# Eight modulation slots as raw matmul products between the mixing output and the feed-forward

## The reference, cut to what matters

```
mod = (silu(c) @ w_mod + b_mod)          # w_mod: 2048 x 12288
sh1, sc1, gt1, sh2, sc2, gt2 = split(mod, 6)
h  = rmsnorm(x) * (1 + sc1) + sh1        # ... mixing: recurrences, gates
x  = x + gt1 * (y @ w_out)               # "mixing output"
h2 = rmsnorm(x, g_norm2) * (1 + sc2) + sh2
u_gate, u_val = split(h2 @ w_up, 2)      # "up", 2 x 5504 columns
x  = x + gt2 * ((silu(conv3x3(u_gate) + conv_b) * u_val) @ w_down)   # "down"
```

## Time and profile before

| | |
|---|---|
| median of 3 runs | 2628.92 us (2626.74, 2628.92, 2629.05) |
| the profiled execution's own time | 2626.53 us |
| its span, first to last instruction | 2624.7 us |
| mean granted clock of TensorE | 0.993 |
| mixing output (16 slots) | 594.6 to 686.0 us of the span |
| `up` (86 slots) | 694.1 to 1175.9 us |
| `down` (44 slots) | from 1175.9 us |

### The profile page before, as it was taken

One profiled execution on the slowest core, in us unless ns is written; L12 is line 12 of the kernel. 1 busy time (PEld: TensorE's weight loads), 2 busy tenths in 40 slices (PEclk: granted clock), 3 DMA queues, 4 the chain that ended last, 5 costly groups with the idle time before them and its releaser, 6 DMA issues.

```text
span 2624.7 us, 41249 instructions
## 1 busy us (share of the span) xinstructions
PE 2567.7 (98%) x15774; PEld 2229.0 (85%) x15774; DVE 1987.9 (76%) x3108; ACT 1322.2 (50%) x1973; POOL 0.2 (0%) x4
## 2 busy tenths in 40 slices
PE   5999999999899999999999999999999999999999
PEld 2687778888788888888888888888888998988888
DVE  4587888978988888888556777777654889567577
ACT  3334434455555555553444544445444655676564
POOL 0000000000000000000000000000000000000000
PEclk8999999999999999999999999999999999999999
DMA  9876675426555555558555555555555444543543
GB/s 399 357 311 259 242 290 206 147 73 243 189 192 184 185 190 192 187 184 314 190 189 185 194 192 187 184 189 193 195 185 187 171 171 178 195 142 117 194 170 134
DMA packets 114256, 530.36 MB, mean 202 GB/s; under 512 B 8224, under 2 KB 8768, under 8 KB 65232
## 3 DMA queue, kind: packets, MB, share of 16 engines
q1 hardware_dynamic: 110448, 507.54, 53.2%
q10 hardware_dynamic: 3680, 21.05, 2.2%
HBM read 526.46 MB, written 2.10 MB: 201 GB/s over the span
## 4 chain that ended last, share of the span: by engine, by line
PE 71%; DVE 8%; ACT 3%; issue 1%; ACTq 0%; DVEq 0%
PE ps L2299 43%; PE ps L2300 22%; DVE lo L1307 3%; ACT hi L622 1%; PE ps L2292 1%; PE ps L2291 1%; PE ps L2290 1%; PE ps L2736 1%; PE ps L2562 0%; ACT p L1263 0%; DVE R L2020 0%; DVE O L2018 0%; PE ps L2596 0%; PE ps L2599 0%; DVE R L2059 0%
## 5 line engine op out<-in xcount | busy, mean ns | idle before, releaser
L1307 DVE TENSOR_TENSOR lo<-raw,hi 128x1024 fp32r<-128x1024 f32 x700 | 827.8, 1221 | 387.9 <-ACT hi L622 387.6
L622 ACT ACTIVATE hi<-raw 128x1024 fp32r<-128x1024 f32 x700 | 709.2, 1055 | 637.0 <-PE ps L2300 605.2
L2299 PE MATMUL ps<-x,hi 128*128 128x512 f32 x1376 | 330.6, 392 | 4.7 <-DVE x L1813 4.7
L2299 PEld LDWEIGHTS ps<-x,hi 128*128 128x128 f32 x1376 | 253.6, 189 | 54.4 <-issue 4.9
L2299 PE MATMUL ps<-y,hi 128*128 128x512 f32 x1024 | 250.6, 392 | 0.7 <-DVE y L1727 0.6
L2299 PE MATMUL ps<-xp,hi 128*128 128x512 f32 x1024 | 244.7, 391 | 0.1
L646 ACT ACTIVATE hi<-raw 128x1024 fp32r<-128x1024 f32 x98 | 103.0, 1058 | 231.8 <-DMA raw<-in_weights 94.2
L2299 PEld LDWEIGHTS ps<-xp,hi 128*128 128x128 f32 x1024 | 188.2, 188 | 36.7 <-ACT hi L622 0.3
L2299 PEld LDWEIGHTS ps<-y,hi 128*128 128x128 f32 x1024 | 186.1, 189 | 35.6 <-issue 1.0
L2300 PEld LDWEIGHTS ps<-x,lo 128*128 128x128 f32 x1376 | 177.1, 192 | 7.0
L2300 PE MATMUL ps<-x,lo 128*128 128x256 f32 x1376 | 179.1, 283 | 0.0
(11 more groups left out here) (396 smaller groups left out, 4197.2 us busy)
## 6 DMA issues: line engine op xcount, KB each, us to landing
raw<-in_weights SPq DMA_DIRECT2D x453, 1024.0 KB, 4.8
wlast<-in_weights ACTq DMA_DIRECT2D x16, 1024.0 KB, 6.0
spare<-in_weights SPq DMA_DIRECT2D x13, 1024.0 KB, 22.2
over_squares<-in_weights SPq DMA_DIRECT2D x9, 1024.0 KB, 16.8
xf<-in_xt SPq DMA_DIRECT2D x4, 1024.0 KB, 9.4
raw<-in_weights SPq DMA_DIRECT2D x4, 768.0 KB, 4.3
R<-in_xt ACTq DMA_DIRECT2D x1, 2048.0 KB, 7.3
out<-R SPq DMA_DIRECT2D x1, 1024.0 KB, 8.6
```

The source lines that it names most:

```text
L622: act.activation(HI[p % PAIR][:, c], RAW[p % RING][:, c], ACT.Copy).then_inc(hi_ready, 1)
L1307: dve.tensor_tensor(LO[p % PAIR][:, c], RAW[p % RING][:, c], HI[p % PAIR][:, c].bitcast(F32), ALU.subtract).then_inc(lo_ready, 1)
L2299: return pe.matmul(o, h, pair[:, :, k, :], start=start, stop=False, **kw)
```

## The change

Groups 12 and 13 (eight slots of gt2) are no longer summed by VectorE. The eight slots go into eight buffers of their own (`wdirect`), each loaded by ScalarE's queue in a turn of its own of the mixing output (`DIRECT_TURNS`). TensorE multiplies them raw, as in `mod_slot`, with a second copy of the window tile (`cwin_again`, made by VectorE in turn 0), into bank 7: two slots ahead of `sum_squares`, six behind it, ahead of `up`. ScalarE copies the bank to `mrows_again` once the operands of `up` are made; `turn_rows(4, mrows_again)` stands ahead of the third slot of `up` and writes to bank 6. VectorE adds the bias at the head of its part of `down`, behind `gp`, and TensorE waits for this at the head of the first slot of `down`, since that slot writes bank 6. `column_sums(12)`, `column_sums(13)` and the two `later_modulation` calls behind the operands go away. The other eight slots are done in `down` as before, numbered anew.

```diff
+DIRECT, LAST = FINAL[:8], FINAL[8:]
+DIRECT_TURNS = (1, 2, 4, 5, 7, 8, 10, 11)
...
+            def load_direct(i):
+                act.dma_start(wdirect[i][:, :], A["weights"][MOD_AT + DIRECT[i]]).then_inc(sem(f"last_loaded{i // 4}"), 16)
...
-            load_final(0)
-            load_final(1)
             split("mix_out", 0, 0)
             for u in range(16):
                 if u:
                     split("mix_out", u // RING, u % RING, 2, range(1 if u == 15 else 2))
-                if u - 1 in FINAL_TURNS[:6]:
-                    load_final(FINAL_TURNS.index(u - 1) + 2)
+                if u in DIRECT_TURNS:
+                    load_direct(DIRECT_TURNS.index(u))
...
+            act.wait_ge(sem("whole_used"), len(WHOLE) + 8)
+            act.activation(mrows_again[:, :], PS[7][:, :], ACT.Copy).then_inc(sem("mod_rows"), 1)
             def ff_silu(j, b):
...
                 if u:
                     n2_sum(u - 1)
-                if u in FINAL_TURNS:
-                    i = FINAL_TURNS.index(u)
-                    final_sum(i)
+                if u == 0:
+                    window(cwin_again)
...
-            later_modulation(12)
-            later_modulation(13)
             own.done(dve.memset(pad[0][:, :], 0.0))
...
+            dve.wait_ge(sem("mod_turned"), 5)
+            for g in range(2):
+                j = 80 + 4 * g
+                dve.tensor_tensor(mview[:, j:j + 4, 0], PS[6][:, 0:32].rearrange("p (q w) -> p q w", w=8)[:, :, 2 * g], v("b_mod", j, 4),
+                                  ALU.add).then_inc(sem("mods_ready"), 1)
             for s in range(4 * DOWN_SLOTS):
...
-            sum_squares("n2", "steps")
-            column_sums(12)
-            column_sums(13)
+            def direct(i):
+                pe.wait_ge(sem(f"last_loaded{i // 4}"), 64)
+                for m in range(4):
+                    lo = (4 * (i % 4) + m) * MW + 2 * (3 - i // 4)
+                    ins = pe.matmul(PS[7][32 * m:32 * m + 32, :], cwin_again[:, lo:lo + 32], wdirect[i][:, 512 * m:512 * m + 512],
+                                    start=i == 0, stop=i == 7, skip_group_check=True)
+                ins.then_inc(sem("whole_used"), 1)
+
+            pe.wait_ge(sem("fold_ready"), 4)
+            pe.wait_ge(sem("mods_ready"), 4 + len(GROUP_ENDS))
+            for i in range(8):
+                if i == 2:
+                    sum_squares("n2", "steps")
+                direct(i)
             for i, r in turns(pe, 2 * KF, lead=1):
...
+                if isinstance(i, int) and i == 0 and r == 2:
+                    turn_rows(4, mrows_again)
...
             for s in range(4 * DOWN_SLOTS):
                 q, j = s // DOWN_SLOTS, 4 * (s % DOWN_SLOTS)
                 units = min(4, KF - j)
+                if s == 0:
+                    pe.wait_ge(sem("mods_ready"), 4 + 14)
```

More of the change, by code:

```diff
@@ L54 @@
 FINAL = [u for u in MODS[7] if u not in SUMMED]
-FINAL_TURNS = (2, 4, 5, 7, 8, 10, 11, 13)
+DIRECT, LAST = FINAL[:8], FINAL[8:]
+DIRECT_TURNS = (1, 2, 4, 5, 7, 8, 10, 11)
 MW = 38
@@ L354, in build @@
                 wk("wsum4", 512, 56), wk("wsum5", 512, 58), wk("wsum6", 512, 112), wk("wsum7", 512, 114)]
-        wlast = [wk("wlast0", SLOT, 0), wk("wlast1", SLOT, 8), wk("wlast2", SLOT, 96), wk("wlast3", SLOT, 104)]
+        wdirect = [wk(f"wdirect{i}", SLOT, (102, 110)[i] if i < 2 else 8 * (i - 2)) for i in range(8)]
+        cwin_again = wk("cwin_again", KD * MW, 48)
+        mrows_again = wk("mrows_again", 512, 51)
+        wlast = [wk("wlast0", SLOT, 96), wk("wlast1", SLOT, 104)]
         tmpx2 = wk("tmpx2", T, 101)
@@ L897, in load_final @@
                     act.wait_ge(sem("mod_summed"), 4 * (NSUM + i) - 4)
-                act.dma_start(wlast[i % 2 + (2 if i >= 8 else 0)][:, :], A["weights"][MOD_AT + FINAL[i]]).then_inc(sem(f"last_loaded{i % 2}"), 16)
+                act.dma_start(wlast[i % 2][:, :], A["weights"][MOD_AT + LAST[i]]).then_inc(sem(f"last_loaded{i % 2}"), 16)
+            def load_direct(i):
+                act.dma_start(wdirect[i][:, :], A["weights"][MOD_AT + DIRECT[i]]).then_inc(sem(f"last_loaded{i // 4}"), 16)
             act.wait_ge(sem("operand_rest"), reached("x", "y", 4))
-            load_final(0)
-            load_final(1)
             split("mix_out", 0, 0)
@@ L973, in _ @@
             act.wait_ge(halves_used, 2 * BASE["down"])
-            load_final(8)
-            load_final(9)
+            load_final(0)
+            load_final(1)
             act.wait_ge(sem("gp_ready"), 1)
@@ L979, in _ @@
                 if 1 <= s < 7:
-                    load_final(s + 9)
+                    load_final(s + 1)
                 q, k = s // DOWN_SLOTS, s % DOWN_SLOTS
@@ L1389, in later_modulation @@
             def later_modulation(g):
-                dve.wait_ge(sem("sums_taken"), g // 2 * 2 + 2 if g >= len(GROUP_ENDS) else g + 1)
+                dve.wait_ge(sem("sums_taken"), len(GROUP_ENDS) + 2 if g >= len(GROUP_ENDS) else g + 1)
                 j = 32 + 4 * g
@@ L1395, in multiplied_sum @@
             def multiplied_sum(i, k, w, pieces):
-                total = sums_of(i // 4)
+                total = sums_of(i // 4 + (len(DIRECT) // 4 if i >= NSUM else 0))
                 for m in pieces:
@@ L1517, in _, with window @@
             dve.memset(ones[:, :], 1.0).then_inc(sem("ones_ready"), 1)
-            own.done(dve.memset(cwin[:, :], 0.0))
-            own.wait()
+            def window(t):
+                own.done(dve.memset(t[:, :], 0.0))
+                own.wait()
+                dve.tensor_copy(t[:, :].rearrange("p (k w) -> p k w", w=MW)[:, :, 6:8],
+                                csil[:, :].rearrange("p (k s) -> p k s", s=2)).then_inc(sem("fold_ready"), 1)
             dve.wait_ge(sem("c_act"), 1)
-            dve.tensor_copy(cwin[:, :].rearrange("p (k w) -> p k w", w=MW)[:, :, 6:8],
-                            csil[:, :].rearrange("p (k s) -> p k s", s=2)).then_inc(sem("fold_ready"), 1)
+            window(cwin)
             dve.wait_ge(sem("eye_loaded"), 16)
@@ L1773, in final_sum @@
             def final_sum(i):
-                dve.wait_ge(sem(f"last_loaded{i % 2}"), 16 * (i // 2 + 1))
-                multiplied_sum(NSUM + i, FINAL[i], wlast[i % 2 + (2 if i >= 8 else 0)], range(4))
+                dve.wait_ge(sem(f"last_loaded{i % 2}"), 64 + 16 * (i // 2 + 1))
+                multiplied_sum(NSUM + i, LAST[i], wlast[i % 2], range(4))
             def n2_sum(u):
@@ L1905, in _ @@
                 if s < 8:
-                    final_sum(s + 8)
+                    final_sum(s)
                 q, k = s // DOWN_SLOTS, s % DOWN_SLOTS
@@ L2457, in mod_slot, with turn_rows @@
                 ins.then_inc(sem("whole_used"), 1)
-            def turn_rows(r):
+            def turn_rows(r, rows=mrows):
                 pe.wait_ge(sem("mod_rows"), r + 1)
@@ L2463, in turn_rows @@
                     for m in range(4):
-                        ins = pe.matmul(PS[6 + r % 2][32 * m:32 * m + 32, 8 * q:8 * q + 8], mrows[:, q * P + 32 * m:q * P + 32 * m + 32],
+                        ins = pe.matmul(PS[6 + r % 2][32 * m:32 * m + 32, 8 * q:8 * q + 8], rows[:, q * P + 32 * m:q * P + 32 * m + 32],
                                         fold[:, :], start=True, stop=True, skip_group_check=True)
@@ L2470, in column_sums @@
                 pe.wait_ge(sem("mods_ready"), 4 + (g // 2 * 2 if g >= len(GROUP_ENDS) else g))
-                pe.wait_ge(sem("mod_summed"), 16 * g + 16)
+                pe.wait_ge(sem("mod_summed"), 16 * (g - (len(DIRECT) // 4 if g >= 14 else 0)) + 16)
                 for q in range(4):
```

## The result

The changed kernel takes 2639.65 us (median of 6 runs, 2638.09 to 2641.59), the kernel before 2628.80 (6 runs): ratio 1.0044, 95% interval 1.0034 to 1.0054, 10.9 us slower. A few single executions of one or the other kernel in the runs of this study took 3.6 to 8.7 ms; they are left out everywhere, the profile of one of them too (the first of the sums put back, which records a granted clock of 1.00 and not the low one that the expectation for its repeat names).

The account below looks back on a forecast made before the run. The prediction took TensorE, at work for 98% of the span, as the bound. Its terms, -0.4 + 0.5 + 9.0 + 2.1 = +11.2 us on the median 2628.9, gave 2640 us, range 2635 to 2644.

Parts of the forecast that it names:

- The sum: Whole kernel: -0.4 + 0.5 + 9.0 + 2.1 = +11.2 us, giving 2640.
- The wait at the head of `down`: First slot of `down`: TensorE stalls for VectorE's bias add, 9.0 us, bounds 8.8 to 9.6.
- The clock behind it: First products of `down` after the stall: low granted clock costs 2.1 us, bounds nothing to 4.2.
- The turn: Third slot of `up`: 16 small products outside any hole cost 0.5 us.
- The earlier operands: Gap ahead of `up`: sum of squares at full clock brings the operands 0.4 us earlier, a gain of 0.4.
- The relief of VectorE: Mixing output: taking 24 us of sums off VectorE gains 0, since TensorE never waits for `LO` there.
- VectorE's chain as the gate: First slot of `up`: VectorE's unbroken work sets when blocks 4 to 7 are ready, so TensorE stands still 2.1 us.
- The rival that I priced too low: First slot of `up`: clock falls in the new 2.1 us hole, adding 2.1 us, 2642.2; chance 0.08.
- The two cited rules: Start of `up`: clock rule alone would give back 2.1 us; third slot: without the drain rule, 0.2 us lower.
- the regained clock: Start of `up`: full clock behind the filled gap gains nothing at the end, as TensorE then waits for VectorE.

Follow-up runs that it names:

- the sums put back: The changed kernel with the bias add moved to the fourth slot of `up` and 32 useless VectorE sums in the old eight mixing output turns; ratio 1.0004.
- the add moved: The changed kernel with VectorE's bias add in the fourth slot of `up`, not at the head of `down`; 2628.74 us, ratio 1.0005.
- the wait alone: The kernel before with one line added: TensorE waits for VectorE's `gp` at the head of the first slot of `down`; 2638.59 us, ratio 1.0041.
- the add first: The changed kernel with VectorE's bias add directly behind the last rest of `up`, ahead of the memsets, `eps2` and `gp`; 2639.94 us, ratio 1.0045.
- the `LO` half moved: The changed kernel with the bias add in `up`'s fourth slot, `turn_rows` ahead of block 4, and VectorE's `LO` half two parts later; 2626.63 us, ratio 0.9994.
- `LO` later on before: The kernel before with only VectorE's 1.2 us `LO` half moved two parts later among the operands of `up`; ratio 0.9999.

## Why the prediction was right, and where it was not

*The sum.* Forecast +11.2 us and 2640; measured +10.9 and 2639.65, and 11.6 between the two profiles. The interval of the ratio reaches from 8.9 to 14.2 us, so that the two numbers lie 0.3 apart is luck; what the profiles bear out is the large terms.

*The wait at the head of `down`*: forecast 9.0, measured 8.98, and shown to be the cause from both sides (the add moved: 1.0005; the wait alone: 1.0041). What it rests on was read rightly: VectorE's order behind the last channel block, at the very times of the earlier trace rows plus 0.2. One bound was off: with adds that cost nothing the stall is 1184.55 - 1175.88 = 8.7 us, not 8.8, and the wait alone measured 8.70.

*The clock behind it*: forecast 2.1, measured 2.38 in the changed kernel, 2.2 in the wait alone, 1.9 in the add first, and gone from the profile once TensorE is kept at work.

*The turn*: forecast 0.5, measured 0.46 (from the last narrow group to the wide products of the third slot it is 708.37 - 706.96 = 1.41 us, where the kernel before has 0.95). In the hole it is free.

*The earlier operands*: forecast -0.4, and the profile has -0.37. As a term it was too generous: it counts only for executions of the kernel before in which the clock had fallen ahead of the sum of squares, and two of the three profiles that have nothing filled into that hole show it full there.

*The relief of VectorE* at 0 is borne out by the sums put back. *VectorE's chain as the gate* is borne out by the `LO` half moved: 1.1 us.

*The rival that I priced too low* is the clock falling behind the new 1.8 us hole. Five profiles have this hole unchanged; four of them show the fall, at 1.6 us each, and the one of the changed kernel, which was the fastest of its six runs, does not. The price (2.1 forecast) and the hole's length (2.1 forecast, 1.8 measured) were near enough, the chance of 0.08 was not. The case that the prediction priced it by, the fall at 688 behind a hole of 2.0 us, is itself one of three: in the wait alone and in `LO` later on before, with the same hole, the clock held until 690, by when TensorE stood in the next one. How often it happens over many runs stays open, and so does how the median can be only 10.9 us up if it is frequent: the scatter from stages that the change doesn't touch is as large.

*The two cited rules.* That activity keeps the clock up (the Trainium skill, TensorE: Matmul & The Clock Gate, Part 1) agrees with the traces: 1.00 from 694 to 698, where before had 0.50. The four falls behind a hole of 1.8 us, which is not a long one, it does not lead one to expect; there the measurement decides. What the prediction held against it stands too: the regained clock ran into the wait for VectorE, 1.81 us, instead of shortening anything. The drain between tiling modes (the Trainium skill, TensorEngine Tiling (Array Packing), Key Properties) can only lie within the 0.46 us of the turn; no run here shows it apart.

## What to carry to other kernels

When a step is taken out of one engine's stream and put elsewhere, look for where its last, tiny part lands: here 0.2 us of adds at the head of a stage, behind 8.5 us of another engine's leftovers, cost 11 us at the seam, and putting them some 460 us earlier took this loss away. Filling a hole on the engine that bounds the kernel pays only up to the next gate that another engine sets; find that gate before counting the gain. For differences of a few microseconds in a long kernel, compare the stretch around the edit in the profiles, not only whole times, which here scattered by up to 4 us; and take more than one profile, since the clock can fall in that stretch in one and not in the next.

## What I had not expected of the hardware

In four of five profiles the granted clock fell to 0.50 behind a hole of 1.8 us; in the one profile that has a hole of 1.35 us it did not. And one and the same stretch of code, the gap of the kernel before, took 23.06 us in one execution and 23.42 in another; in the first the clock was still full when the sum of squares ran (0.70 us), in the second it had just fallen (1.06 us).
